# Attention with split turned heads, late low parts, column-grouped sample rows, and stores and caches on GpSimd's queue

## The reference

```python
for i in range(DEPTH):                       # 2 layers
    for grp in range(2):                     # prompt (512 rows), sample (32 rows)
        sh1, sc1, gt1, sh2, sc2, gt2 = adaln(cs[grp], w_ada[i], b_ada[i])
        h = modulate(rms_norm(x, norm_mix[i]), sh1, sc1)
        if i == 0:                           # gated linear attention, 4 heads, chunks of 64
            mix, S_fin = gla_mixer(h, S0, ...)
        else:                                # differential attention, 8 heads of two 64-wide parts
            q, k, v = diff_project(h, ...)   # rms-normed q and k
            o = diff_attend(q, k, v, ...)    # a = softmax(q0 k0) - lam * softmax(q1 k1); o = a @ v
            o = rms_norm(o, diff_norm) * (1 - lam_init)
            mix = o @ diff_w_out
        x = x + gt1 * mix
        h = modulate(rms_norm(x, norm_ffn[i]), sh2, sc2)
        f, conv = conv_ffn(h, ...)           # up, causal conv of width 3, silu gate, down
        x = x + gt2 * f
```

## Time and profile before

| | us |
|---|---|
| median of 3 runs | 1517.7 |
| lowest, highest | 1513.07, 1521.38 |
| profiled execution, its time | 1515.08 |
| its span, first to last instruction | 1513.3 |
| busy: TensorE, VectorE, ScalarE, GpSimd | 1439.0, 829.5, 650.6, 65.3 |

### The profile page before, as it was taken

The page is one execution under the profiler, slowest core; times in us unless marked ns, Lnnn a source line. Parts: engine busy times, 40 slices in busy tenths (PEclk is TensorE's granted clock), DMA queues, the critical chain, the costliest instruction groups (busy, mean ns, idle before and its releaser), DMA issues.

```text
span 1513.3 us, 26783 instructions
## 1 busy us (share of the span) xinstructions
PE 1439.0 (95%) x11308; PEld 1343.6 (89%) x11308; DVE 829.5 (55%) x1330; ACT 650.6 (43%) x1431; POOL 65.3 (4%) x98
## 2 busy tenths in 40 slices
PE   5899999999999999999999999989789999999999
PEld 3778888889999999999887777778779999999999
DVE  4433442537767866868554544465565554555454
ACT  4323332436555245252454554562355553452431
POOL 0000000030000000000200000000200000000000
PEclk9999999999999999999999999999999999999999
DMA  9143242253333533524712030321412222222222
GB/s 385 69 139 109 98 150 91 91 196 112 112 112 112 174 130 108 201 100 130 265 72 86 29 113 29 107 72 49 167 57 87 100 79 90 93 70 98 78 79 102
DMA packets 35545, 171.82 MB, mean 114 GB/s; under 512 B 3793, under 2 KB 8145, under 8 KB 23522
## 3 DMA queue, kind: packets, MB, share of 16 engines
q1 hardware_dynamic: 25362, 127.11, 24.1%
q0 software_dynamic: 10064, 43.01, 7.8%
HBM read 162.19 MB, written 7.91 MB: 112 GB/s over the span
## 4 chain that ended last, share of the span: by engine, by line
PE 87%; DVE 5%; ACT 4%; issue 3%; DMA 1%; POOL 1%; POOLq 0%; SPq 0%; DVEq 0%; ACTq 0%
PE ps L535 26%; PE ps L537 25%; PE ps L536 25%; ACT w_hi L983 2%; PE ps L618 1%; PE ps L885 1%; DVE w_lo L1399 1%; PE ps L923 1%; DVE h_lo L1448 1%; POOL acc L500 1%; DVE sq L1441 1%; PE ps L625 1%; PE ps L842 1%; PE ps L630 1%; PE ps L729 1%
## 5 line engine op out<-in xcount | busy, mean ns | idle before, releaser
L535 PE MATMUL ps<-h_hi,w_hi 128*128 128x272 f32 x2176 | 638.7, 294 | 18.8 <-DVE h_lo L1448 9.7
L537 PE MATMUL ps<-h_hi,w_lo 128*128 128x272 f32 x2176 | 631.8, 290 | 0.0
L536 PE MATMUL ps<-h_lo,w_hi 128*128 128x272 f32 x2176 | 628.6, 289 | 0.0
L535 PEld LDWEIGHTS ps<-h_hi,w_hi 128*128 128x128 f32 x2176 | 412.3, 189 | 32.1 <-issue 14.1
L536 PEld LDWEIGHTS ps<-h_lo,w_hi 128*128 128x128 f32 x2176 | 412.9, 190 | 1.2 <-issue 1.2
L537 PEld LDWEIGHTS ps<-h_hi,w_lo 128*128 128x128 f32 x2176 | 411.7, 189 | 0.0
L1399 DVE TENSOR_TENSOR w_lo<-w_raw,w_hi 128x2048 fp32r<-128x2048 f32 (+2 forms) x109 | 226.6, 2079 | 155.5 <-ACT w_hi L983 155.2
L983 ACT CAST w_hi<-w_raw 128x2048 fp32r<-128x2048 f32 (+2 forms) x109 | 188.3, 1728 | 221.6 <-PE ps L537 220.5
L536 PE MATMUL ps<-act_lo,w_hi 128*128 128x272 f32 (+1 forms) x704 | 203.9, 290 | 0.0
L535 PE MATMUL ps<-act_hi,w_hi 128*128 128x272 f32 (+1 forms) x704 | 203.3, 289 | 0.0
L537 PE MATMUL ps<-act_hi,w_lo 128*128 128x272 f32 (+1 forms) x704 | 203.2, 289 | 0.0
(11 more groups left out here) (223 smaller groups left out, 1457.3 us busy)
## 6 DMA issues: line engine op xcount, KB each, us to landing
w_raw<-in_wst SPq DMA_DIRECT2D x73, 1024.0 KB, 4.8
w_raw<-in_wst SPq DMA_DIRECT2D x28, 768.0 KB, 4.2
a_raw<-in_ada_r POOLq DMA_DIRECT2D x32, 512.5 KB, 3.8
a_raw<-in_ada_w POOLq DMA_DIRECT2D x24, 512.0 KB, 5.0
a_gap<-in_ada_w POOLq DMA_DIRECT2D x12, 1024.0 KB, 10.3
a_pro<-in_ada_w SPq DMA_DIRECT2D x8, 1024.0 KB, 18.4
w_raw<-in_wst SPq DMA_DIRECT2D x8, 512.0 KB, 4.1
xT<-in_xT SPq DMA_DIRECT2D x4, 544.0 KB, 6.5
```

The lines of the kernel that those rows point to most:

```text
L535: mm(out, lhs_hi, rhs_hi, start=first, stop=False)
L536: mm(out, lhs_hi, rhs_lo, start=False, stop=False)
L537: return mm(out, lhs_lo, rhs_hi, start=False, stop=last)
```

## The change

In words:

- Turned heads: ScalarE's `heads_turned` writes the high part straight to `od_hi` (or `h_hi` for the last pair), and VectorE's new `heads_low` writes the low part to `od_lo` (`h_lo`) from the same PSUM bank. `oT2` and its two further passes are gone. `doutA` reads `od_hi` and `od_lo` and waits for `od_out`.
- Low parts: in the attention stage `evacuate(u, False)` leaves out `low`, which is owed and done after `weights_out`. At the start of GLA `low(2)` moves behind the third unit of `v`.
- Fillers: pair 2 uses `DIFF_STEPS`, so it has one unit less; the last pair has `LAST_STEPS`; four units of `doutA` are kept for the end (`TAIL_A`), two ahead of the last turns and two behind them. The high part of `doutB` is made before the last turned heads.
- Sample rows: `h_smp` and `h_smp2` hold the sum of high and low part of the 32 sample columns in plain fp32, and `sample_rows` makes 16 plain fp32 matmuls, slice k on column group k % 4. The four partial sums stay apart on the 128 partitions of `v_r` and `vd`; the keys' turning, the scores and the weights are made four times over, so that the next product adds them up. For the store the value rows are folded by a product with `fold` and copied to `vfs`.
- Queues: key and value stores and cache loads are issued by GpSimd, and the four memsets for the mask move to just ahead of attention. `pr` lies in `a_raw`.

```diff
+LAST_STEPS = [1, 1, 2, 2, 2, 2, 2, 2, 1]
...
+DOUT_B = block_units(("doutB", 0))
+TAIL_A = 4
...
 def diff_fill(p):
-    us = block_units(("dv", p))[2 if p < NPAIR - 1 else 3:]
+    us = block_units(("dv", p))[2:]
     if p + 1 < NPAIR:
-        us = us + block_units(("dk", p + 1)) + block_units(("dq", p + 1)) + block_units(("dv", p + 1))[:2 if p + 2 < NPAIR else 3]
-        steps = DIFF_STEPS if p + 2 < NPAIR else [2, 2, 2, 2, 2, 1, 1, 1, 1]
+        us = us + block_units(("dk", p + 1)) + block_units(("dq", p + 1)) + block_units(("dv", p + 1))[:2]
+        steps = DIFF_STEPS
     else:
-        us = us + DOUT_A[:13]
-        steps = [1, 1, 1, 2, 2, 2, 2, 2, 2]
+        us = us + DOUT_A[:-TAIL_A]
+        steps = LAST_STEPS
...
@@ gpsimd
+            def cache_in(p):
+                if p >= 2:
+                    pool.wait_ge(av_ok, NU * (p - 2) + NU)
+                pool.dma_start(kcT[:, p % 2], A["kcT"][:, 2 * p:2 * p + 2, :]).then_inc(kc_in[p % 2], 16)
+                pool.dma_start(vc[:, p % 2], A["vc"][p]).then_inc(kc_in[p % 2], 16)
...
+            cache_in(0)
+            cache_in(1)
+            for p in range(NPAIR):
+                keys_out(p)
+                if 1 <= p < NPAIR - 1:
+                    cache_in(p + 1)
+                values_out(p)
             pool.wait_ge(od_turned, 3 * NPAIR)
@@ tensor
+            def sample_rows(u):
+                n = UNITS[u][0]
+                x = h_smp if BL[n][0] == "v" else h_smp2
+                pe.wait_ge(smp_ok, 1 if BL[n][0] == "v" else 2)
+                for term, w in enumerate(w_parts(n)):
+                    for k in range(KT):
+                        j = k % 4
+                        ins = mm(ps[TS * j:TS * (j + 1), U_BANK[u], 0:BC], x[:, k, :], f32(w[:, k, :]),
+                                 start=(term == 0 and k < 4), stop=(term == 1 and k >= 4), skip_group_check=True)
+                ins.then_inc(unit_done, 1)
...
-                ins = pe.transpose(ps[0:TS, 6, 0:P], kd[:, s, TP:T], ident)
+                for j in range(4):
+                    ins = mm(ps[TS * j:TS * (j + 1), 6, 0:P], kd[:, s, TP:T], ident, start=True, stop=True)
...
+                    for jj in range(2):
+                        ins = mm(ps[jj * TS:(jj + 1) * TS, 6, EV:2 * EV], fold, vd[:, s, NPR, jj * EV:(jj + 1) * EV], start=True, stop=True,
+                                 skip_group_check=True)
...
-            units(DOUT_A[13:])
+            units(DOUT_A[-TAIL_A:-TAIL_A + 2])
             turn_heads(NPAIR - 1, 0, 4)
             turn_heads(NPAIR - 1, 1, 5)
             turn_heads(NPAIR - 1, 2, 6)
+            units(DOUT_A[-TAIL_A + 2:])
             units(block_units(("doutB", 0)))
@@ scalar
+            split(BN[("doutB", 0)])
             heads_turned(NPAIR - 1, 0, 4)
             heads_turned(NPAIR - 1, 1, 5)
             heads_turned(NPAIR - 1, 2, 6)
-            act.wait_ge(od_out, 3 * NPAIR)
-            output_hi(oT2, 6)
-            output_hi(oT2, 7)
-            evacuate_all(DOUT_A[13:])
+            evacuate_all(DOUT_A[-TAIL_A:])
@@ vector
             v0 = block_units(("v", 0))
-            evacuate_all(block_units(("qk", 0)))
             evacuate(v0[0])
             evacuate(v0[1])
             gates(0)
             evacuate(v0[2])
+            low(2)
             evacuate(v0[3])
...
+            def heads_low(p, part_, bank):
+                dve.wait_ge(od_hi_ok, 3 * p + part_ + 1)
+                hi, lo, k = (od_hi, od_lo, 2 * p) if p < NPAIR - 1 else (h_hi, h_lo, KA)
+                if part_ < 2:
+                    STT(out=lo[:, k + part_, 0:TP], in0=ps[:, bank, :], scalar=st[:, 1:2], in1=f32(hi[:, k + part_, 0:TP]),
+                        op0=ALU.mult, op1=ALU.subtract).then_inc(od_out, 1)
...
-                    if len(todo[i]) > 1:
-                        evacuate(todo[i][0])
-                    if last and i == 2:
-                        for k in range(2, KA):
-                            output_lo(oT2, 4, k)
+                    for u in todo[i][:-1]:
+                        evacuate(u, False)
+                        owed = UNITS[u][0] + 2 if u == LAST_U[UNITS[u][0]] else owed
                     weights_out(gu)
-                    evacuate_all(todo[i][-1:])
+                    if p and 1 <= i < (3 if last else 4):
+                        heads_low(p - 1, i - 1, 7)
+                    if owed is not None:
+                        low(owed)
+                        owed = None
...
             outputs_normalised(NPAIR - 1)
-            evacuate_all(DOUT_A[13:])
-            output_lo(oT2, 4, 6)
-            output_lo(oT2, 4, 7)
+            evacuate_all(DOUT_A[-TAIL_A:-TAIL_A + 2])
+            heads_low(NPAIR - 1, 0, 4)
+            heads_low(NPAIR - 1, 1, 5)
+            heads_low(NPAIR - 1, 2, 6)
+            low(owed)
+            evacuate_all(DOUT_A[-TAIL_A + 2:])
```

More of the change, by code:

```diff
@@ L300, in hybrid_stream_step @@
         osq = sb("osq", [P, EV], c=d)
+        vfs = sb("vfs", [2 * TS, 2, EV], c=d)
+        h_smp2 = sb("h_smp2", [P, KT, TS], c=d)
         d.close()
@@ L708, in keys_and_scores @@
                     mm(ps[:, 3, c], ke[:, s, c], qe[:, s, c], start=True, stop=True)
-                mm(ps[0:TS, 6, P:P + TS], ke[:, s, TP:T], qe[:, s, TP:T], start=True, stop=True).then_inc(att_ok, 1)
+                for j in range(4):
+                    ins = mm(ps[TS * j:TS * (j + 1), 6, P:P + TS], ke[:, s, TP:T], qe[:, s, TP:T], start=True, stop=True)
+                ins.then_inc(att_ok, 1)
             def state_terms(h, pair):
@@ L946, in _ @@
                     scores(gu + 2)
-                    if last and i in (1, 2):
-                        turn_heads(p - 1, 2 * i - 2, 7)
-                    elif p and not last and 1 <= i < 4:
+                    if p and 1 <= i < (3 if last else 4):
                         turn_heads(p - 1, i - 1, 7)
@@ L1033, in evacuate @@
                 if kind not in ACT_KINDS:
[L1034 removed]
+                    if u == LAST_U[n] and then_split:
                         split(n + 2)
@@ L1349, in _ @@
                     gu = NU * p + i
-                    if last and i in (1, 2):
-                        heads_turned(p - 1, 2 * i - 2, 7)
-                    elif p and not last and 1 <= i < 4:
+                    if p and 1 <= i < (3 if last else 4):
                         heads_turned(p - 1, i - 1, 7)
-                    if last and i == 2:
-                        act.wait_ge(od_out, 3 * p)
-                        for k in range(2, KA):
-                            output_hi(oT2, k)
                     for idx in NORM_FIRST.get(i, []):
@@ L1362, in _ @@
                     exps(gu + 2)
-                    evacuate_all(todo[i][-1:])
+                    for u in todo[i][-1:]:
+                        evacuate(u, not (last and i == NU - 1))
                     for idx in NORM_THEN.get(i, []):
                         head_norms(p + 1, idx)
-                    if last and i == 1:
-                        heads_turned(p - 1, 1, 7)
-                        act.wait_ge(unit_done, LAST_U[BN[("dv", p)]] + 1)
-                        output_hi(oT2, 0)
-                        output_hi(oT2, 1)
+                    if last and i == 2:
+                        heads_turned(p - 1, 2, 7)
                     values_out(gu)
                 output_roots(p)
+            split(BN[("doutB", 0)])
             heads_turned(NPAIR - 1, 0, 4)
@@ L1551, in _ @@
             low(1)
+            dve.wait_ge(alow_ok, 1)
+            dve.wait_ge(h_ok, KT)
+            TT(h_smp[:, :, :], f32(h_hi[:, :, TP:T]), f32(h_lo[:, :, TP:T]), ALU.add).then_inc(smp_ok, 1)
             def gates(h):
@@ L1727, in _ @@
             dve.wait_ge(lam_loaded, 16)
+            dve.wait_ge(h_ok, KT * 4)
+            TT(h_smp2[:, :, :], f32(h_hi[:, :, TP:T]), f32(h_lo[:, :, TP:T]), ALU.add).then_inc(smp_ok, 1)
             lp = lam_in[:, :, :].rearrange("p (a b) d -> p a b d", b=2)
@@ L1934, in _layout @@
     part("selm")[row, TS * (row // (2 * TS)) + row % TS] = 1.0
+    part("fold")[row, row % TS] = 1.0
+    part("smask")[:] = (row % TS)[:, None] <= np.arange(TS)[None, :]
     A["cst"] = cst
```

179 lines of the change are left out of this document (94 added, 85 removed).

## The result

The changed kernel takes 1480.3 us in the median of four runs (1477.3 to 1480.8) against 1517.6 (1513.1 to 1521.4) for the kernel before: a ratio of 0.975 (95% interval 0.972 to 0.978), 37.3 us less. The forecast was 1486, 31.8 us less.

A forecast was written before the change was run, and what follows sets the result against it. TensorE, busy 95% of the span, bounds the kernel through its work and waits. Terms gained 37.7 us and lost 5.9, so 31.8 less: 1483.3 from the profiled execution, 1486 from the median; own range 1479 to 1493, 8 in 10 1477 to 1500.

The forecast's parts named there:

- A: Start of GLA: copying `v` before block 2's low part removes TensorE's wait and the slow clock behind it; 5.0 us gained.
- B: Eight sample-row units: 16 plain fp32 matmuls over four overlapping column groups replace 24 matmuls; 7.0 us gained.
- C: Pairs 0 to 2, second and fourth steps: copying `aT` before the weights' low part removes six waits; 9.0 us gained.
- D: Last pair: splitting turned heads straight from PSUM and deferring weights' low parts removes four waits; 9.6 us gained, 1.0 kept back.
- E: End of attention: new order of units, turns and low parts removes the `h_lo` wait and slow clock; 7.1 us gained.
- last steps' waits: Last steps of pair 2 and the last pair: one unit less each brings waits costing 0.9 and 1.0 us.
- added matmuls: Fourfold key turning, scores and weights plus folding, in four heads and the pairs: 3.0 us lost, bounds 0 and 6.
- change of mode: Sample units: old ones taken to pay the tiling-mode drain already; if only new ones paid, the gain would be 5.6 us.
- rival in which stalls move: Added splits and deferred low parts meet on VectorE, above all in the last pair; 1499 us, chance 0.15.
- kept-back 1.0 us: Last pair: held back because the first output units want turned heads' low parts with 0.4 us or less to spare.
- slow clock behind the split of `oT2`: Last pair: lowered granted clock behind the second wait costs 2.1 us, gone once no second pass is left.
- one wait of 1.7 us: End of attention: TensorE stands for a bank VectorE empties late, after the next block's low part; 1.7 us lost.

The follow-up runs named there:

- e1: Changed kernel with VectorE's low part of block 2 ahead of the first copy of `v` again; 1484.8 us.
- e10: Changed kernel with sample units again as 24 matmuls, the four copies kept, and six VectorE zero fills placed behind the work that ScalarE's first-key copies wait for; 1486.7 us.
- e4: Changed kernel with low parts of weights ahead of the copy of `aT` again in pairs 0 to 2; 1495.3 us.
- e2: Changed kernel with the eight sample units again as 24 matmuls, the four copies kept, its zero fills bringing a wait for `kT`; 1490.5 us.
- e3: Changed kernel with sample units again as 24 matmuls and without the four copies, its zero fills bringing a wait for `kT`; 1487.2 us.
- e6: Changed kernel with all four last `doutA` units ahead of the last turns, VectorE taking the weight block before the heads; 1482.2 us.
- e7: Changed kernel with VectorE's low part of the last up projection's first block moved behind all copies of the `doutB` units; 1482.0 us.

## Why the prediction was right, and where it was off

The time, 1480.3, lies in the range and 5.7 us under the forecast; the gain was 37.3 us against 31.8, or 34.4 from one profiled run to the other. So by the traces the sum missed 2.6 us of gain; another 2.8 come from the choice of executions, as the profiled one lay 2.5 us under the median before and 0.3 above it after. By terms, forecast and what the runs showed:

| term | forecast | measured | from |
|---|---|---|---|
| A, start of GLA | 5.0 | 5.2 | e1 |
| B, sample rows | 7.0 | 5.7 | e10 |
| C, pairs 0 to 2 | 9.0 | 10.2: 3.6, 3.6 and 3.0 | e4 in pair 0, before's waits |
| D and E, less the last steps' waits | 13.8 | 15.0 | rest of before's steps |
| added matmuls | -3.0 | -1.0 | e2 and e10 against e3, traces |

D and E with the two waits of 0.9 and 1.0 us come from before's steps behind the first cache step of pair 2: 17.1 us to the column sums, less 1.5 for C's one wait there (the fourth step of pair 2) and 0.65 for the last pair's sample unit and copies. The terms make 35.1 us, the traces 34.4. Behind 805 us the traces show 25.9 and the terms there 25.5; ahead of it, in the stretches that vary, they show 8.5 and the terms 9.6.

- A was right in place, size and sign that was named (no wait ahead of the third unit, granted clock 1.00).
- B's mechanism, overlapping groups, was right and is shown by the serial order. Its size was off by the change of mode, which row 89.92 of the earlier trace rows had shown and which was taken to be paid by the old units as well.
- C's waits were sized right, 1.5 us each. A third block's end in the seventh step of pairs 0 and 1 was not counted (0.32 us idle in the kernel before, 0.6 lost). What the late low parts do for the turned heads was not seen either. With direct splits and the old order pairs 1 and 2 would have taken 10.5 us more than now, of which 1.6 are slow clock, and not 6.6, so the two edits of VectorE's order lean on each other. The rival in which stalls move describes that kernel, not this one.
- D's kept-back 1.0 us was not needed. The two waits at the last steps came as said (0.94 and 1.17 us from start to start). The slow clock behind the split of `oT2` was sized about right: it lasts beyond the output unit, and the same values and scores take 3.18 us there in place of 2.14. With the unit's matmuls, 0.23 us apart in place of 0.12 or 0.13, that is 2.3 us against the 2.1 forecast. TensorE's timelines, before and after:

```profile
1022.43 1.48 PE L923 MATMUL ps<-vd,aT 128*128 128x128 f32 x6
...
1025.61 0.40 PE L535 MATMUL ps<-h_hi,w_hi 128*128 128x272 f32 x1
```

```profile
998.51 0.94 PE L963 MATMUL ps<-vd,aT 128*128 128x128 f32 x6
...
1000.65 0.39 PE L548 MATMUL ps<-od_hi,w_hi 128*128 128x272 f32 x1
```

- E's clock of units, turns and low parts held to half a microsecond, down to the one wait of 1.7 us; the four loads stayed hidden. Its slow clock, put at 1.6 us (three quarters of 2.0 are 1.5), was 1.8. But that two of the units stand behind the turns, which the sum counted on as cover, matters little, and with all four ahead of them e6 does without heads ahead of the weight block too. Whether the direct split, ScalarE's early high part or the fourth unit carries the term is open.
- The added matmuls are the term that was furthest off. They were priced at 0.4 us a head, and they take 0.46; but they had a cover that the prediction didn't name, the waits for `a_raw`. In the pairs, priced at 0.35, the wider forms give back most of what they add, and 0.1 is left. With C and the unneeded 1.0 of D this is why the terms made less than the traces show; B's error went the other way and hid a part of it.

## What to carry to other kernels

In a list worked off in order, ask of each deferrable operation what stands behind it and who waits for that; here moving low parts of weights behind a 0.4 us copy was worth 3.6 us in a pair, and 4.3 and 6.2 where other short work shared the list, the 6.2 with a slow clock behind the wait. When one wait goes, look at what starts beside the work that now sets the time: an edit that gave nothing gave 2.1 us once a GpSimd sum and a VectorE subtraction no longer ran side by side. To price an edit, compare the distance between the same two instructions in two traces, which was good to 0.1 us here, from 805 to 1064 us, where medians were good to 3; look at the granted clock of both traces first, which moved single steps by 1.3 to 3.1 us. And list all that an edit moves before you read what came of it: e6 moved units on TensorE and, on VectorE, the weight block ahead of the heads, and the second shows that the gain does not need heads ahead of the block.

## What the runs showed of the hardware

- A GpSimd sum of 128x544 took 3.47 us in place of 1.36 while VectorE subtracted two SBUF tensors, and 1.36 beside VectorE work that reads PSUM and one SBUF tensor (e7).
- Behind two equal waits of TensorE of 2.41 us in one trace (e4) the granted clock was 0.57 over the next 4 us once and 1.00 once.
- fp32 instructions of 256 columns on 32 columns of the array start 0.22 us apart in one column group; with four groups in turn 16 start in 0.89 us, and with groups one after another the next group starts after four instructions of the one before, two side by side.
- Entering and leaving the four-group form cost 0.18 and 0.05 us; 24 fp32r matmuls on 32 columns of one group did not, while two plain fp32 instructions on 32 columns of one group started 0.21 us behind the one ahead in place of 0.11 (e3).
- Four small products over 128 rows of the array took 0.22 us, and over 32 rows 0.34 us, with the 16 products ahead of them 0.1 us longer too (0.99 against 0.90; e3 and e10).
